# Unpermuted rows with strided transposes, and a mixer factor folded into the pooling weights

## The reference, cut to what matters

```python
def pool_mixer(h, w_pool, pool_scale):
    ...
    outs.append(pooled.astype(h.dtype) @ w_pool[g])      
    return jnp.concatenate(outs, axis=-1) * pool_scale

x = x + g_m * y
h = rmsnorm(x, norm_ffn_g[l]) * (1 + sc_f) + sh_f
y = hier_moe(h, ...)
x = x + g_f * y
```

## Time and profile before

| | |
|---|---|
| Median of 3 runs | 1866.48 us |
| The profiled execution | 1867.46 us |
| Its span, first to last instruction | 1865.7 us |
| TensorE busy, matmuls | 1648.7 us, 88% |
| VectorE busy | 1567.1 us, 84% |
| ScalarE busy | 1030.0 us, 55% |
| DMA | 547.60 MB, 294 GB/s on average |
| Mean granted clock of TensorE | 0.932 |

### The profile page before, as it was taken

One profiled execution on the slowest core, in us unless ns is written; L12 is line 12 of the kernel. 1 busy time (PEld: TensorE's weight loads), 2 busy tenths in 40 slices (PEclk: granted clock), 3 DMA queues, 4 the chain that ended last, 5 costly groups with the idle time before them and its releaser, 6 DMA issues. The chain is left out here.

```text
span 1865.7 us, 20029 instructions
## 1 busy us (share of the span) xinstructions
PE 1648.7 (88%) x7821; PEld 1367.8 (73%) x7821; DVE 1567.1 (84%) x1153; ACT 1030.0 (55%) x838; POOL 424.7 (23%) x230
## 2 busy tenths in 40 slices
PE   3799998996599999999999858659999999999980
PEld 3577786785478888888888748648888888888870
DVE  4977685544599999999999859659999999999976
ACT  6221213122277777777777524327777777777742
POOL 1422221430313223323233100002232222232210
PEclk9799999896699999999999979769999999999995
DMA  9689722114389999999999935138999999999957
GB/s 331 210 300 316 272 85 85 46 46 181 134 325 378 376 383 384 393 382 385 381 392 388 388 141 207 53 109 324 380 385 385 392 386 384 385 384 388 392 204 277
DMA packets 125269, 547.60 MB, mean 294 GB/s; under 512 B 24003, under 2 KB 42975, under 8 KB 76021
## 3 DMA queue, kind: packets, MB, share of 16 engines
q1 hardware_dynamic: 91934, 497.98, 70.7%
q0 software_dynamic: 18432, 33.60, 4.7%
q10 hardware_dynamic: 14808, 14.73, 2.3%
HBM read 533.61 MB, written 46.17 MB: 311 GB/s over the span
## 5 line engine op out<-in xcount | busy, mean ns | idle before, releaser
L1276 DVE TENSOR_TENSOR unit_low<-unit,unit_high 128x2048 fp32r<-128x2048 f32 x384 | 856.0, 2283 | 27.3 <-ACT unit_high L907 26.7
L907 ACT ACTIVATE unit_high<-unit 128x2048 fp32r<-128x2048 f32 x384 | 735.3, 1915 | 36.7 <-DMA unit<-in_moe_w_up_dram 13.6
L1567 PE MATMUL ps<-unit_high,block_columns_high 128*128 128x512 f32 x1024 | 408.6, 399 | 9.5 <-DVE block_columns_low L1281 9.5
L1569 PE MATMUL ps<-unit_high,block_columns_low 128*128 128x512 f32 x1024 | 402.5, 393 | 0.0
L1568 PE MATMUL ps<-unit_low,block_columns_high 128*128 128x512 f32 x1024 | 402.4, 393 | 0.0
L704 POOL DMA_INDIRECT expert_rows<-y_out,assignment x64 | 179.7, 2808 | 833.2 <-DVE y_out L1308 820.3
L1567 PEld LDWEIGHTS ps<-unit_high,block_columns_high 128*128 128x128 f32 x1024 | 194.4, 190 | 49.6 <-DVE block_columns_low L1281 10.8
L1569 PEld LDWEIGHTS ps<-unit_high,block_columns_low 128*128 128x128 f32 x1024 | 194.4, 190 | 41.8
L1568 PEld LDWEIGHTS ps<-unit_low,block_columns_high 128*128 128x128 f32 x1024 | 194.7, 190 | 39.0
L1579 PE MATMUL ps<-unit_high,act_columns_high 128*128 128x512 f32 x512 | 206.7, 404 | 9.8 <-DVE unit_low L1276 9.8
L1581 PE MATMUL ps<-unit_high,act_columns_low 128*128 128x512 f32 x512 | 201.6, 394 | 0.0
(11 more groups left out here) (228 smaller groups left out, 2033.7 us busy)
## 6 DMA issues: line engine op xcount, KB each, us to landing
unit<-in_moe_w_gate_dram SPq DMA_DIRECT2D x128, 1024.0 KB, 7.5
unit<-in_moe_w_up_dram SPq DMA_DIRECT2D x128, 1024.0 KB, 7.2
unit<-in_moe_w_down_dram SPq DMA_DIRECT2D x128, 1024.0 KB, 8.4
cond_w<-in_w_ada_dram SPq DMA_DIRECT2D x80, 512.0 KB, 5.4
y_in<-expert_rows SPq DMA_DIRECT2D x16, 1024.0 KB, 7.2
x_rows<-in_x_dram SPq DMA_DIRECT2D x8, 1024.0 KB, 9.9
cond_w<-in_w_ada_dram SPq DMA_DIRECT2D x8, 1024.0 KB, 11.0
in_w<-in_w_in_even_dram ACTq DMA_DIRECT2D x12, 512.0 KB, 7.5
```

Of the source, the lines that this page charges most:

```text
L907: a.activation(high[k][:, :], raw[i % SLOTS][:, :], ACT.Copy).then_inc(unit_high, 1)
L1276: v.tensor_tensor(low[i % SLOTS][:, :], raw[i % SLOTS][:, :], high[k][:, :].bitcast(F32), ALU.subtract)\
L1567: mm(dst, xT_hi[:, q, :], high[k][:, cols], start=q == 0, stop=False)
L1569: last = mm(dst, xT_lo[:, q, :], high[k][:, cols], start=False, stop=q == KD - 1)
```

## The change

1. `entry_rows` and `gated_up` write their results in the natural order. A new helper, `strided_to_columns`, transposes every eighth column of the rows (a step of 32 bytes), and `act_transpose` reads every fourth column of the activations (16 bytes). It is used for the normed rows, for the gathered rows, and in the branch for further blocks. The transposes of x at the start stay as they are.
2. The multiplication by grow[0] (L1395) is left out of the stage between the expert phases. In its place `pool_columns` multiplies pool_w by it, one tensor_tensor over 128x2048, in VectorE's stream of layer 0's third expert between `activation_rows` and `low_part_of_rows`. TensorE waits for that (`pool_scaled`) where it waited for pool_w.
3. `load_y` waits for `c_ss`, raised by ScalarE after the square that uses the y buffer as scratch, in both layers.

```diff
@@ load_y (SP)
                 if t >= YB:
-                    if l == 0:
-                        sp.wait_ge(x_mixed1, t - YB + 1)
-                    else:
-                        sp.wait_ge(c_ss, NT + t - YB + 1)
+                    sp.wait_ge(c_ss, l * NT + t - YB + 1)
@@ entry_rows (VectorE)
-                v.tensor_tensor(xn[t % 2][:, :].rearrange("p (k q) -> p q k", q=P),
-                                tmp_row[l][:, :].rearrange("p (q k) -> p q k", k=KD),
-                                b_ffn[l][:, :].rearrange("p (q k) -> p q k", k=KD), ALU.add).then_inc(xn_ready, 1)
+                v.tensor_tensor(xn[t % 2][:, :], tmp_row[l][:, :], b_ffn[l][:, :], ALU.add).then_inc(xn_ready, 1)
@@ gated_up (VectorE)
-                return v.tensor_tensor(act_r[:, :].rearrange("p (k q) -> p q k", q=P),
-                                       BANK[1].rearrange("p (q k) -> p q k", k=KF),
-                                       sig[:, :].rearrange("p (q k) -> p q k", k=KF), ALU.mult)
+                return v.tensor_tensor(act_r[:, :], BANK[1], sig[:, :], ALU.mult)
@@ VectorE
+            def pool_columns():
+
+                dve.wait_ge(pool_loaded, 16)
+                dve.wait_ge(rows1_loaded, 16)
+                v.tensor_tensor(pool_w[:, :, :, :], pool_w[:, :, :, :],
+                                bc(grow[0][:, :].rearrange("p (g n) -> p g n", n=PD).unsqueeze(2), [P, PG, 2, PD]),
+                                ALU.mult).then_inc(pool_scaled, 1)
@@ moe (VectorE)
                     activation_rows(n)
+                    if n == 2:
+                        pool_columns()
@@ between the expert phases (VectorE)
-                    tmp = y_in[t % YB][:, 0, :]
-                    ch.link(v.tensor_tensor(tmp, PA[1], grow[0][:, :], ALU.mult))
-                    v.tensor_tensor(xr[:, t, :], xr[:, t, :], tmp, ALU.add).then_inc(x_mixed1, 1)
+                    v.tensor_tensor(xr[:, t, :], xr[:, t, :], PA[1], ALU.add).then_inc(x_mixed1, 1)
@@ TensorE
+            def strided_to_columns(dst, src):
+
+                by_k = src[:, :].rearrange("p (q k) -> p k q", k=KD)
+                for k in range(KD):
+                    last = nc.tensor.transpose(dst[:, k * P:(k + 1) * P], by_k[:, k, :], ident[:, :])
+                return last
@@ entry_T, block_T, and the further blocks with xg_x (TensorE)
-                rows_to_columns(PT, xg[n % 2]).then_inc(b_T, 1)
+                strided_to_columns(PT, xg[n % 2]).then_inc(b_T, 1)
@@ act_transpose (TensorE)
+                by_q = act_r[:, :].rearrange("p (s q) -> p q s", q=KF)
                 for q in range(KF):
-                    last = nc.tensor.transpose(PM[:, q * P:(q + 1) * P], act_r[:, q * P:(q + 1) * P], ident[:, :])
+                    last = nc.tensor.transpose(PM[:, q * P:(q + 1) * P], by_q[:, q, :], ident[:, :])
@@ before the stage between the expert phases (TensorE)
             pe.wait_ge(bands_ready, 1)
-            pe.wait_ge(pool_loaded, 16)
+            pe.wait_ge(pool_scaled, 1)
```

More of the change, by code:

```diff
@@ L349, in hybrid_trunk @@
         consts = sem("consts")
-        bands_ready = sem("bands_ready")
+        bands_ready, pool_scaled = sem("bands_ready"), sem("pool_scaled")
         dve_chain, act_chain, pool_chain = sem("dve_chain"), sem("act_chain"), sem("pool_chain")
@@ L1493, in entry_T @@
                     pe.wait_ge(n_T_kept, n)
-                rows_to_columns(PT, xn[t % 2]).then_inc(n_T, 1)
+                strided_to_columns(PT, xn[t % 2]).then_inc(n_T, 1)
             def entry_logits(l, t):
@@ L1643, in moe @@
                             pe.wait_ge(m["xg"], 16 * j + 16)
-                            rows_to_columns(PT, xg_x).then_inc(m["pe"], 1)
+                            strided_to_columns(PT, xg_x).then_inc(m["pe"], 1)
                             pe.wait_ge(m["act"], 3 * j + 1)
```

## The result

The changed kernel takes 1856.36 us (median of 5 runs, 1854.65 to 1858.73) against 1867.3 of the kernel before beside it (5 runs, 1862.36 to 1868.59): a ratio of 0.9948, 95% interval 0.9936 to 0.996. It is 0.5% faster, where the forecast was 3% slower. The profiled execution has a span of 1857.0 us (1865.7 before) and a mean granted clock of 0.935 (0.932).

What follows compares the result with a forecast made beforehand. TensorE was taken to bound the experts, VectorE the stage between. Loads +67.0, layer 0's entry +2.2, stage between -7.3 and first experts -0.8 gave +61.1 on 1867.46, so 1928.6 us, range 1851 to 1948.

Steps and rivals of the forecast that it cites:

- The load's price: Strided transposes in both layers' experts: 1.68 ns per column, trains at 0.215 us instead of 0.108, +67.0 us in all.
- the room: Transposes' weight loads: 58 ns hide behind 108, so a load may become 1.9 times slower, to 0.84 ns per column, unseen.
- the strided load stays hidden: Rival for all transposes: loads up to 0.84 ns per column leave trains at 0.108 us; -14.7 us, 1852.8 us; chance 0.31.
- only the rows pay: Rival for the transposes: the activations' 16-byte step is free, only the rows' loads cost; about 1908 us; chance 0.08.
- The experts' pace: Both expert phases: TensorE sets the pace, 17.7 us per expert; whatever VectorE saves there only lengthens its waits.
- The stage between: Between the expert phases: TensorE becomes the bound; -7.3 us with slow trains, -12.4 with unchanged transposes.
- the clock 3.4: End of the stage between: a shorter gap keeps TensorE's clock up, router matmuls at 0.109 instead of 0.214, 3.4 us gained.
- the train 0.8: End of the stage between: with unchanged transposes the last train also speeds up, 0.8 us gained.
- Layer 0's entry: Trains of tiles 0 to 4 add 3.7 us, shorter VectorE stores return 2 x 0.73: +2.2 us with slow trains.
- The moved multiply: pool_columns on VectorE in layer 0's third expert: 2.45 us of work, taken as covered, 0; 2.45 once if not.
- the y loads: Layer 0's y loads start some microseconds earlier, but nothing waits for them or is held back: 0.
- The first experts': First expert of each layer, where TensorE waits for act_rows: L1286's shorter store gives -0.8 us; elsewhere in the experts it is hidden.

Runs made afterwards that it cites:

- the table of steps: A kernel of its own timing loads, matmuls and copies at steps of 1 to 32 elements; 24 transposes took 2.78 us at step 1, 3.06 at 4, 2.78 at 8.
- the multiplication alone: The kernel before with only the multiplication moved into pool_w and the y loads' new wait, rows still permuted by VectorE's stores: 1861.63 us, ratio 0.9972.
- the strides alone: The kernel before with only the unpermuted stores and the strided transposes, L1395's multiplication and the y loads' wait as before: 1866.31 us, ratio 0.9998.
- the late y loads: The changed kernel with layer 0's y loads waiting for the residual again: 1856.02 us, ratio 0.9937.

## Why the prediction was wrong

**The load's price: the step that failed.** In the sum this is the term of +67.0 us. The forecast bounded a column between 0.84 ns, up to which nothing is lost, and about 1.8, and took 1.68 because VectorE's writes and its reduction agreed on it, "which looks like a rate of the memory and not of the engine". The ground was not there: the prediction says that the engine differs between the two, but both groups of rows are VectorE's, so they agree as rates of VectorE alone. Its additions at a step of 8 elements measure 0.7 ns per element more than adjacent ones, here too:

```profile
L63 DVE TENSOR_TENSOR vector_drain<-data,other x6: 284/285/293, 259.0 to 260.0; 128x128 f32<-128x128 f32 x6
...
L73 DVE TENSOR_TENSOR vector_drain<-data,other x6: 376/378/382, 266.3 to 267.7; 128x128 f32<-128x128 f32 x6
```

A transpose's load at that step takes (188 - 82) / 128 = 0.83 ns per column, and one at 4 elements 1.0. The spacing moved from 0.108 to 0.110 (rows) and 0.118 (activations) instead of 0.215, and in place of +67.0 us the experts measured +2.8 (0.2 and 2.6 in the table above), not all of it the loads'. Two things were to be had from the rows. The two loads of the earlier trace rows already showed that a transpose's load is a kind of its own, twice as fast per column as an ordinary one, which spoke against carrying over an absolute rate from another engine. A factor would have served here: VectorE's 1.8 over 1.06 ns, on 0.45, is 0.76 ns per column, below the 0.84 of the room. And the room was reckoned as a factor of 1.9, while the loads became slower by 1.8 (rows) and 2.2 (activations): the one sits just inside, the other just outside, which is what their trains show.

By the Trainium skill (Advanced Engine Details and Errata, SBUF Cachelines) every access that goes to another line pays. By that rule both steps pay, and the loads' rows agree, 188 and 210 ns for 140; the ordinary loads agree as well, 329 and 335 for 192. The prediction also took from it that two hits on a line hide the access. At a step of 2, where a line is hit twice, that is so for ordinary loads (196 ns) and not for transposes' (209). What the rule does not say is that the payment can be hidden, and the time is decided by that.

**The rival "the strided load stays hidden"**, held at 0.31, is what happened: 1852.8 forecast, 1856.4 measured. Against the traces, -14.7 was forecast and the spans differ by -8.7. Of these 6.0 us, 3.6 lie in the experts (-0.8 forecast, +2.8 measured), 1.5 in the stage between, and the rest in stretches that the change does not touch. The rival's condition was a load no slower than 0.84 ns per column; the rows have 0.83, the activations 1.0, and their trains do pay a little, 0.63 us for 0.60. The second reading behind the rival "only the rows pay", that four fp32 elements are the free reach (the Trainium skill, SBUF — State Buffer, section Door 1), is wrong by the table of steps for what a transpose shows: 4 is its slowest step, 212 ns for 140.

**The experts' pace.** Right, and now shown by doing the trains twice: TensorE sets it, VectorE's saving only lengthens its waits. A difference remains, 0.02 us per expert in layer 0 and 0.06 in layer 1. Of it 0.02 to 0.03 are the activations' trains, as the kernel with the activations read side by side shows. The rest is open: where the rows are read side by side the period is 17.69 or 17.73 us in a layer, now one and now the other from trace to trace, so what one compares with moves by 0.04 itself. The 2.8 us of the table are also not all period. In layer 1 the 31 periods give 1.4, and 1.1 lie behind the last expert's train, where the kernel before takes 35.3 us and the one with the multiplication alone, whose loads are adjacent too, 36.8. And two other traces with the same strided trains (the strides alone, and the late y loads) take 623.3 us for routing and experts of layer 1, where the changed kernel's trace has 625.46 and the kernel before 622.84.

**The stage between.** Forecast -12.4 with unchanged transposes, measured -10.9. Pace 9.7, measured 9.69; the gap before the last transposes "about 1 us", measured 0.88; the clock 3.4 and the train 0.8, measured 3.2 and 0.8. The term off is the start of the last transposes, 8.2 earlier forecast, 6.9 measured from the last down matmul (100.03 for 106.96), most of it because a mixer product in the changed kernel's trace ran at a lower clock (5.31 us for 3.70 at 1121.66; the kernel before has such a one too, at 5.12, where VectorE sets the pace) and moved the tiles behind it. That the short gap keeps the clock was in part luck: the late y loads' trace, with the same gap, lost it.

**Layer 0's entry.** +2.2 was forecast with slow trains, -1.5 with unchanged ones; measured -1.4. **The moved multiply** and **the y loads**: 0 forecast, 0 measured. **The first experts'** -0.8: the wait for act_rows did shrink, from 0.80 and 0.87 us to 0.43 and 0.50, but the next wait, for the low part of the second expert's rows, grew from 2.28 and 2.49 to 2.55 and 2.76, so 0.2 is left.

## What to carry over

A rate measured on one engine is not a rate of the memory; here a factor would have carried over and the rate did not. How much slower a step makes an access has to be set against what that very operation hides behind. When parts of a change don't add up, read the granted clock stretch by stretch before looking for an interplay of the parts. And where TensorE waits for a chain of other engines, short matmuls in the wait were worth 18 us here, more than the change itself; look in the trace whether each group of them did what it was put there for.

## What the runs showed of the hardware that was not expected

- A transpose's load of 128 fp32 columns takes 140 ns, an ordinary fp32 or float32r load of as many 192. At any step of 2 elements or more the first takes 187 to 212. The second takes 196 at a step of 2, 261 at 3, and 329 to 337 at 4 and 8.
- The moving side pays at once. Float32r matmuls of 512 columns read at a step of 2 take twice as long as adjacent ones, 12 in 5.59 instead of 2.92 us, and steps of 3, 4, 5 and 8 are the same within 6%:

```profile
212.34 2.92 PE L185 MATMUL ps<-data_r 128*128 128x512 f32 x12
...
217.82 5.59 PE L188 MATMUL ps<-data_r 128*128 128x512 f32 x12
...
250.61 5.33 PE L200 MATMUL ps<-data_r 128*128 128x512 f32 x12
```

That is at a granted clock of 1.00. Of what was timed, only the transposes' loads hide a step of 8: the moving side and the ordinary loads lose half their rate.

- Gaps of about 1 us leave TensorE's clock open. Before the last transposes the granted clock stayed at 1.00 after 0.88 us in three traces and fell to 0.50 after 0.89 in a fourth; after 1.6 us it fell in both traces that had such a gap there. Of the mixer products that follow an idle time of 1.11 or 1.12 us, in the nine traces without fillers at that place, 13 of 27 ran partly at the low level (5.2 to 5.6 us) and 14 at 1.00 (3.7). So single traces of one and the same stage differ by several us.
